# Two-layer hybrid decoder trunk on one core: attention's transposes moved into the projection, fewer modulation tiles ahead of the norm, decay rows split in two, and the second layer's w2 products as three single passes

## The reference

```python
for l in range(DEPTH):                                        # DEPTH = 2
    mod = (silu(c) @ w_ada[l] + b_ada[l])[:, None, :]         # w_ada: 1024 x 6144
    sh1, sc1, g1, sh2, sc2, g2 = jnp.split(mod, 6, axis=-1)
    u = layer_norm(x) * (1.0 + sc1) + sh1
    z = u @ w_in[l]                                           # 2920 columns, four head groups
    y_a = mla_mixer(...)          # 4 heads, latent attention, width 96
    y_b = mlstm_mixer(...)        # 4 heads, q k^T times exp(decay), causal
    y_c = short_conv_mixer(...)   # b * conv3(c * h), 256 channels
    y_d = diff_attn_mixer(...)    # 4 heads, two softmax maps each, width 32
    mix = jnp.concatenate([y_a, y_b, y_c, y_d], axis=-1) @ w_out[l]
    x = layer_norm(DN_ALPHA * x + g1 * mix) * ln1_g[l] + ln1_b[l]
    u2 = layer_norm(x) * (1.0 + sc2) + sh2
    ffn = grouped_moe(u2, w_router, b_router, w1[l], w3[l], w2[l])
    #     16 experts of hidden width 256: w2[e] @ (silu(w1[e] u) * w3[e] u), top 2 of one group of 4
    x = layer_norm(DN_ALPHA * x + g2 * ffn) * ln2_g[l] + ln2_b[l]
```

## Time and profile before

| what | value |
|---|---|
| median of 3 runs | 805.85 us (802.21 to 807.32) |
| the profiled execution: its own time | 810.88 us |
| its span, first to last instruction | 809.0 us |
| TensorE busy | 682.6 us (84%) |
| VectorE busy | 570.6 us (71%) |
| ScalarE busy | 331.4 us (41%) |
| GpSimd busy | 71.9 us (9%) |
| mean granted TensorE clock | 0.916 |
| DMA over the span | 192.39 MB, 238 GB/s |

### The profile page before, as it was taken

One profiled execution on the slowest core, in us unless ns is written; L12 is line 12 of the kernel. 1 busy time (PEld: TensorE's weight loads), 2 busy tenths in 40 slices (PEclk: granted clock), 3 DMA queues, 4 the chain that ended last, 5 costly groups with the idle time before them and its releaser, 6 DMA issues.

```text
span 809.0 us, 9622 instructions
## 1 busy us (share of the span) xinstructions
PE 682.6 (84%) x3630; PEld 543.7 (67%) x3630; DVE 570.6 (71%) x808; ACT 331.4 (41%) x511; POOL 71.9 (9%) x40
## 2 busy tenths in 40 slices
PE   1379898989549899999964999899866899999991
PEld 1379886769448566676644998776866666666650
DVE  6796986565878676766559998656577767665527
ACT  0154445630244544545223455374045444544510
POOL 3001000530100000000112000044010000000001
PEclk9998999889759999999975999989976999999996
DMA  9979977005614899999690993530152789998811
GB/s 347 380 230 318 315 259 285 2 1 183 255 58 153 293 396 368 396 376 380 227 366 19 311 375 151 183 130 1 53 201 112 257 293 410 359 383 307 276 53 54
DMA packets 81701, 192.39 MB, mean 238 GB/s; under 512 B 10984, under 2 KB 42984, under 8 KB 81644
## 3 DMA queue, kind: packets, MB, share of 16 engines
q1 hardware_dynamic: 75240, 184.73, 62.4%
q10 hardware_dynamic: 6408, 6.96, 2.9%
HBM read 190.60 MB, written 1.05 MB: 237 GB/s over the span
## 4 chain that ended last, share of the span: by engine, by line
PE 72%; DVE 15%; issue 4%; DMA 3%; ACT 3%; POOL 2%; POOLq 0%; ACTq 0%; SPq 0%; DVEq 0%
PE bank L1823 21%; PE bank L1876 13%; PE bank L1543 11%; PE bank L1541 7%; PE bank L1697 2%; PE bank L1910 2%; DVE mod_acc L945 2%; DMA ada_ring<-in_w_ada 1%; DVE st L956 1%; POOL rstd L585 1%; DMA ada_open<-in_w_ada 1%; DVE e_lo L1046 1%; PE bank L1807 1%; DVE us_rest L1420 1%; PE bank L1507 1%
## 5 line engine op out<-in xcount | busy, mean ns | idle before, releaser
L1046 DVE TENSOR_TENSOR e_lo<-e_ring,e_hi 128x2048 fp32r<-128x2048 f32 x64 | 146.6, 2291 | 76.4 <-ACT e_hi L657 76.4
L657 ACT ACTIVATE e_hi<-e_ring 128x2048 fp32r<-128x2048 f32 x64 | 122.1, 1908 | 2.3 <-DMA e_ring<-in_w 2.3
L1876 PE MATMUL bank<-e_ring,hT 128*128 128x512 f32 x256 | 115.3, 593 | 2.3 <-ACT hT L875 2.3
L1823 PE MATMUL bank<-e_hi,us_hi 128*128 128x512 f32 x256 | 102.0, 406 | 0.0
L1823 PE MATMUL bank<-e_hi,us_lo 128*128 128x512 f32 x256 | 98.9, 395 | 0.0
L945 DVE SCALAR_TENSOR_TENSOR mod_acc<-ada_ring,c_col,mod_acc 128x1024 f32<-128x1024 f32 x59 | 74.2, 1281 | 21.2 <-DMA ada_ring<-in_w_ada 21.2
L1876 PEld LDWEIGHTS bank<-e_ring,hT 128*128 128x128 f32 x256 | 48.1, 189 | 51.1 <-issue 49.1
L1543 PE MATMUL bank<-w_hi,u_hi 128*128 128x256 f32 (+2 forms) x224 | 66.6, 297 | 8.3 <-DVE u_lo L1065 7.2
L1823 PE MATMUL bank<-e_lo,us_hi 128*128 128x512 f32 x256 | 69.8, 395 | 0.0
L1543 PE MATMUL bank<-w_lo,u_hi 128*128 128x256 f32 (+2 forms) x224 | 66.0, 295 | 0.0
L1543 PE MATMUL bank<-w_hi,u_lo 128*128 128x256 f32 (+2 forms) x224 | 65.8, 294 | 0.0
(11 more groups left out here) (267 smaller groups left out, 1392.4 us busy)
## 6 DMA issues: line engine op xcount, KB each, us to landing
e_ring<-in_w SPq DMA_DIRECT2D x128, 512.0 KB, 5.9
e_ring<-in_w SPq DMA_DIRECT2D x32, 1024.0 KB, 8.1
ada_ring<-in_w_ada SPq DMA_DIRECT2D x59, 512.0 KB, 8.1
w_ring<-in_w_in SPq DMA_DIRECT2D x20, 1024.0 KB, 8.0
ada_open<-in_w_ada SPq DMA_DIRECT2D x37, 512.0 KB, 8.8
w_ring<-in_w_out SPq DMA_DIRECT2D x8, 1024.0 KB, 5.0
w_ring<-in_w_in SPq DMA_DIRECT2D x2, 1056.0 KB, 5.8
ln_gb<-in_ln_g ACTq DMA_DIRECT2D x4, 512.0 KB, 4.1
```

The source lines that it names most:

```text
L657: nc.scalar.activation(e_hi[slot][:], e_ring[E_RAW[c % len(E_RAW)]][:], ACT.Copy).then_inc(e_hi_ready, 1)
L1046: V.tensor_tensor(e_lo[slot][:], e_ring[slot][:], e_hi[E_HIGH[c % len(E_HIGH)]][:].bitcast(F32), ALU.subtract).then_inc(e_lo_ready, 1)
L1823: return pe.matmul(dst, u[:, k, cols], w[:, :, k % (KC // 2), :], start=start, stop=stop)
L1876: mm = pe.matmul(bank[banks[half]][:, :], hT[:, c * P:(c + 1) * P], w[:, c, half * 512:(half + 1) * 512], start=(start and c == 0), stop=( ...
```

## The change

1. `turn_rows` moves behind tile 10, and `turn_diff` and `turn_qk` between the two halves of tile 11; `turn_qk` writes other banks. `gate_rows` goes behind `scores(1)`. ScalarE's and VectorE's parts move along. The convolution is cut into five steps, one behind each of the pairs 0 to 4.
2. `ADA_EARLY` is 5. Three of the tiles go where the eight stood, two between the first and second half of `post_norm` for t = 0. Layer 1 takes 5 of its 8 `gate2` tiles there as well and the other three with experts 0 to 2. In layer 0 eleven go with experts 8 to 15, two each with 13 to 15.
3. The decay rows are split into `rows_hi` and `rows_lo`, and the float32 product with `head_sel` becomes two fp32r products with a broadcast column of the identity. The banks of the score pairs swap, so that map 12 waits for ten exponentials and map 13 for twelve.
4. W_out's fourth low part moves from GpSimd to VectorE, behind pair 5; its four high pieces (12 to 15) follow piece 11 directly on ScalarE.
5. In layer 1 w2 and hT are split: `down_high` on ScalarE, `down_low` and `hidden_low` on VectorE, and `expert_down` runs 12 single-pass matmuls in place of 4 float32 ones. `down_hi` lies over `mod_acc`, `down_lo` in the slot of w2 itself.

The core of the diff; banks, buffer addresses and semaphore counts are left out.

```diff
-ADA_EARLY = 8
+ADA_EARLY = 5
...
+def ada_beside(l, e):
+    late = ADA_FIRST - ADA_EARLY if l < DEPTH - 1 else 0
+    done = 0 if l < DEPTH - 1 else ADA_EARLY
+    double = max(0, late - (N_EXP - KC))
+    lo = done + e + max(0, e - (N_EXP - double))
+    hi = lo + (2 if e >= N_EXP - double else 1)
+    return range(ADA_AT["last", l] + lo, ADA_AT["last", l] + min(hi, KC + late))
...
         def score_bank(at):
-            return (0 if at // 2 % 2 else 2) + at % 2
+            return (2 if at // 2 % 2 else 0) + at % 2
...
                 root(2, slice(0, 8))
-                out_low(W_OUT_TILES - 1)
...
+            def down_high(l, e):
+                act.wait_ge(*arrivals["down", l, e])
+                if e >= 2:
+                    act.wait_ge(*layer_view(l)(down_done, e - 1))
+                nc.scalar.activation(down_hi[e % 2][:], e_ring[E_DOWN[e % 2]][:, 0:2 * D].rearrange("p (c n) -> p c n", c=2),
+                                     ACT.Copy).then_inc(down_hi_ready, 1)
...
+                        if step == 2 * NW_IN - 1:
+                            d_out_all()
+                            turned_queries_out()
                         act.wait_ge(*Y(z_done, step + 1))
...
-                    if n == 11:
-                        d_out_all()
+                    if n == 10:
+                        rows_and_lambda()
...
-                    out_high(at)
+                    for piece in range(at, at + 1 if at < 11 else 16 if at == 11 else at):
+                        out_high(piece)
...
+                split_down = l == DEPTH - 1
+                if split_down:
+                    act.wait_ge(*Y(row2_done, 4))
+                    act.wait_ge(*Y(rows_g, 2))
+                    down_high(l, 0)
...
                         turned_out(e)
                         if 2 * e + 4 < N_CHUNKS:
                             up_high(l, 2 * e + 4)
+                        if split_down and e + 1 < N_EXP:
+                            down_high(l, e + 1)
...
                 for half in range(2):
+                    if t == 0 and half == 1 and gate == 0:
+                        for i in ada_early(l)[ADA_SLOTS:]:
+                            ada_step(i)
                     half_done(t, half)
...
+                decays = rows[:, :, :].rearrange("p a b -> p (a b)")[:, P:4 * P]
+                link(V.tensor_copy(rows_hi[:], decays))
+                V.tensor_tensor(rows_lo[:], decays, rows_hi[:].bitcast(F32), ALU.subtract)
...
+                    if p <= 4:
+                        conv_step(p)
...
                     if p == 5:
                         diff_out(1)
+                        dve.wait_ge(*Y(out_hi_ready, W_OUT_TILES * W_OUT_PIECES))
+                        V.tensor_tensor(w_lo[3][:, :, 0:256], w_ring[3][:, :, 0:256],
+                                        w_hi[W_OUT_HIGH[3]][:].bitcast(F32)[:, :, 0:256], ALU.subtract).then_inc(out_lo_last, 1)
...
-                    for i in range(ADA_EARLY):
-                        ada_step(ADA_AT["next"] + i)
+                for i in ada_early(l)[:ADA_SLOTS]:
+                    ada_step(i)
...
+                split_down = l == DEPTH - 1
+                if split_down:
+                    down_low(0)
...
                             up_low(l, 2 * e + 3)
                         if e % 4 == 0 and e > 0:
                             group_out(e // 4 - 1)
+                        hidden_low(e)
                         if 2 * e + 4 < N_CHUNKS:
                             up_low(l, 2 * e + 4)
-                        ada_beside(e)
+                        if split_down and e + 1 < N_EXP:
+                            down_low(e + 1)
+                        ada_steps(e)
...
-                    for i in range(2):
-                        causal(bank[2 * i])
                     for i, h in enumerate(heads):
-                        pe.matmul(bank[2 * i][:, 0:384], head_sel[:, h * P:(h + 1) * P], decays, start=False, stop=True)
+                        pe.wait_ge(*(Y(p_act, 10 + 2 * i) if p == 6 else Y(decay_ready, i + 1)))
+                        causal(bank[2 * i])
+                        for q, part in enumerate((rows_hi, rows_lo)):
+                            pe.matmul(bank[2 * i][:, 0:384], head_r[:, h:h + 1].to_broadcast([NH, P]), part[:, :], start=False, stop=(q == 1))
...
+                if split_down:
+                    pe.wait_ge(down_hi_ready, e + 1)
+                    passes = ((hT_hi, down_hi[e % 2]), (hT_lo, down_hi[e % 2]), (hT_hi, down_lo[E_DOWN[e % 2]]))
...
+                        if n == NW_IN - 1 and half == 1:
+                            turn_diff()
+                            turn_qk()
                         w_step(l, n, half)
...
-                    if n == 11:
-                        turn_diff()
+                    if n == 10:
                         turn_rows()
-                pe.wait_ge(*Y(z_out, 21))
-                turn_qk()
-                gate_rows()
                 for p in range(NPAIR + 2):
                     if p < NPAIR:
                         scores(p)
+                    if p == 1:
+                        gate_rows()
```

218 lines of the change are left out of this document (126 added, 92 removed).

## The result

After the change the kernel takes 819.71 us (median of 4 runs, 812.62 to 824.98); the kernel before, on the same chip, 804.17 (802.21 to 807.32). The ratio is 1.017, with an interval of 1.012 to 1.022; it leaves out the longest of the four, which fell in a slower state of the chip (817.88 is the median of the other three). The prediction was 782.2.

A forecast was written before the change was run, and what follows sets the result against it. TensorE, busy 84% of the span and 72% of the chain, was taken to bound the kernel where it arrives last. 810.9 - 16.4 - 8.3 + 1.1 = 787.3; from the median, 805.85 - 23.6 = 782.2 us; range 768 to 797.

The forecast's parts named there:

- Part 5: Layer 1's experts: single-pass w2 products, TensorE's saving mostly taken by a new two-expert load loop; +1.1 us net.
- load 4.9: Layer 1's w2 loop: each w2 load lands in 4.9 us, within 18.2 us for two experts.
- rivals D: Layer 1's w2 loop: landings of 6 to 7 us add some 10 us, with rival C besides; 799 us, chance 0.08.
- rival E: Layer 1's w2 loop: landings stay 8.4 us and the clock falls; +29 against -24.7, 810 us, chance 0.04.
- the start costs: Layer 1's first experts: early low parts delay 3.4 us, expert 3's queued load 2.7 us.
- -5: Layer 1's experts: TensorE's work beside the loop, scatter and second gate's rows, gains 7.2 us, of which 5 counted.
- Parts 2 and 3: Attention, both layers: low part off GpSimd gives 2.5 us a layer; split decays 1.4, less 0.2 for splitting rows.
- The convolution's steps fit VectorE's gaps: Opening of attention: the convolution steps fit because VectorE is busy only 4.04 of 9.60 us.
- rival C: Attention: GpSimd holds the moved low part and the clock stays low; gain 5 us a layer, 788.6 us, chance 0.16.
- The decays and the clock: Attention, per layer: split decay product brings the last pair's products 1.4 us earlier; fewer TensorE waits raise the clock, 1.5.
- Parts 1 and 4: Opening of attention: first scores 3.7 us earlier, 3.0 net a layer; layer 0's norm: last half 8.3 us earlier.
- The sum: Whole kernel: attention 16.4 us over both layers and norm 8.3 gained, layer 1's experts +1.1; 23.6 us off the median.

The follow-up runs named there:

- both passes moved: Changed kernel with part 5 undone, convolution's five steps behind pairs 0 and 1, fourth low part behind the last y_lo: 793.4 us, ratio 0.986.
- the runs that had each alone: Kernel before with only the fourth low part moved to VectorE behind the last y_lo: 803.2 us, 0.998; with only part 4's modulation tiles: 796.53 us, 0.993.

## Why the prediction was wrong, step by step

**Part 5 failed, in two terms.** The loop of two experts was drawn rightly, "followed from the end of one expert's down products", and the trace after shows it link by link; "load 4.9" was mis-sized. It came from a load at 754.42 us, late in the layer, and stood for all. The landings on the chain are 9.1, 7.2, 6.8 and 6.7 us up to 727 us, so that two experts take 20.2 us and not 18.2. The text had a longer landing in its rivals D ("landings of 6 to 7 us") and E ("it decides from landings of about 8 us on"), and argued against E that landings fall to 4.9 once the modulation tiles end. The trace of the kernel before already shows otherwise. Its last modulation tile was issued at 703.05; this is the w2 load issued at 714.76, behind it (DMA issues of before, 714.5 to 715.5 us):

```profile
e_ring<-in_w SPq DMA_DIRECT2D x1, 1024.0 KB, 7.0
```

The next, at 723.89, took 7.0 as well, and only those from 735.30 on took 4.9 to 5.2. Nor does a long landing need the uneven traffic of the loop: in the fastest version on SyncE's queue, where the experts follow evenly, w2 landed after 5.5 to 8.5 us from 640 to 732 us, and no wait for it is on the chain.

The second term is "the start costs", 3.4 + 2.7 = 6.1 us. By the start of expert 4's up products the changed kernel has lost 11.8 us (16.5 + 25.9 against 12.4 + 18.3, in the chains). The clock falls are in it, which the forecast left to rival E: the up products of experts 1, 2 and 4 take 7.20, 7.46 and 6.47 us for 5.47, together 4.7. From there to the start of expert 15's the change loses 2.5 us against the version with w2 unsplit, where the forecast, with its "-5", had a gain; and from there to the end another 2.0, for which the forecast had no term (expert 15 too waits there for its w2: 4.88 us to land, then the high pass). Together part 5 costs 15 to 16 us and not 1.1.

**Parts 2 and 3 failed in attention.** "The convolution's steps fit VectorE's gaps" counted VectorE's busy time (4.04 of 9.60) and not GpSimd's in the same row, 4.52 us: a step in a gap is no use where GpSimd's pass fills that gap. The text held this very thing against the low part (rival C), and did not ask it of the convolution, whose operations are of the same kind. By the Trainium skill ("GPSIMD Engine Reference", 1. Specifications) an instruction with two SBUF inputs on VectorE contends with GpSimd for shared interfaces; L1254 and L1360 are both of that kind, so the trace agrees, with 3.71 us for 0.87 and 4.65 for 2.29. For the low part the forecast had 0.4 us if it is held and 2.9 if not, and took 1.4 a layer; the held case came. Moving both gives 10 us, and by the profiles that is the low part's gain; the convolution met the pass again.

**The decays and the clock** were 1.4 and 1.5 us a layer. No gain of the split shows in the times. The low stretches stayed as long as TensorE idled there: granted clock 0.83 and 0.73 from 148 to 170 us after, 0.64 and 0.70 in the earlier trace rows. From 158 us on it came to 1.00 with the low part moved (0.83 from 138 to 158 us even there).

**Parts 1 and 4 were right**: the first scores 3.9 us a layer nearer in the traces for 3.7, and the norm's last half at TensorE's end. Part 4 measured 6.0 us for 8.3, within its interval.

**The sum.** The parts without w2 were to give 24.7 us. They give 1.4 as written, and 11.1 with both passes moved. Of the 13.6 that are missing even then, part 2 is some 3 and part 4 some 2, by the runs that had each alone. The sum had no term for the convolution held 4.2 us a layer. The decays (2.8) and the clock (3.0) no run isolates well enough to say. So the rest stays open.

The fastest version is the one with w2 split late, its third pass last and the low part clear of GpSimd: 0.982 of before, or 0.979 with the w2 loads on ScalarE's queue. The split of w2 is not where its gain is shown to come from; the version without it is at 0.986.

## What to carry to other kernels

When a buffer's reader is moved ahead, draw the loop that starts at the release of the buffer and give the load its longest landing, not its shortest: here the landing went from 4.9 to 9.1 us with what else was in flight, and it can be read off the kernel before at the same place in its stream. When work is moved to an idle engine, look at what its neighbours do in those same microseconds; here two operations of 0.9 us cost 3.7 if GpSimd has a pass under way, and moving them earlier only made another one meet it. Look at the trace after such a move before crediting it. Cost the beginning of a pipeline on its own: most of the loss here fell in the first four of sixteen experts.

## What the runs showed of the hardware

**VectorE beside GpSimd looks stopped, not slowed.** The 4.65 us of the low part are 2.5 up to the end of GpSimd's pass and 2.1 behind it, with 2.29 of work. The operation of 0.69 us that took 4.91 ended 0.55 behind the pass (143.92 against 143.37), and line 1243 of before 0.55 behind its own. So each did some 0.14 us of its work at the start and all the rest when the pass was over, however long the pass still had. The first of the two convolution operations (L1254) took 3.31 us for 0.48 and ended 0.3 behind. VectorE's other operations in the same stretch, which read a bank of PSUM, were of their usual length (L1343, 0.55 us). The chain of waits calls the stop "issue".

**A long landing is not cured by another queue.** Up to some 760 us, with at least two other loads in flight at its issue, 1 MB landed after 5.5 to 10.0 us on ScalarE's queue (issued at once) and after 5.3 to 9.1 us on SyncE's (the changed kernel); with at most one in flight it was 4.9 to 5.0 us on either.

**The clock decides 4 us of a projection by chance.** The first 288 matmuls of layer 0's projection took 35.4 to 35.9 us in nine of the sixteen profiles and 39.1 to 39.9 in seven, and layer 1's first 336 took 41.0 to 41.5 in nine and 45.5 to 45.7 in seven, with the same code. Busy time by stretch at the start of layer 0's projection, of the kernel before and of the one with the fourth low part moved:

```profile
40.00:45.00 5.00, 0.32 (x3) 0.22 (x2) 4.25 (x12) 4.30 (x13) 0.00 (x0) 1.00 1.07 385
...
60.00:65.00 5.00, 5.00 (x26) 5.00 (x26) 4.93 (x15) 1.86 (x3) 2.80 (x2) 0.53 0.90 306
```
```profile
40.00:45.00 5.00, 0.32 (x2) 0.21 (x2) 4.33 (x12) 4.39 (x13) 0.00 (x0) 0.50 1.06 381
...
60.00:65.00 5.00, 5.00 (x45) 5.00 (x44) 4.93 (x15) 1.98 (x3) 2.82 (x2) 1.00 1.05 387
```

TensorE was all but idle ahead of both. In the first the clock fell in the middle of the projection, to 0.79 and 0.53 from 55 to 65 us, though TensorE was busy without a gap there (0.50 is 1.2 GHz, 1.00 is 2.4). All seven long profiles show such a fall, and none of the nine short ones. The clock ahead of the projection doesn't decide it: of the seven profiles in which it was at 1.00 from 40 to 45 us three are short, and of the nine in which it was at 0.50 three are long. Why it falls the profiles don't show. Two such places make 8 us between executions of one kernel, which is why stages, and not whole spans, were compared, and why the differences below 1% above carry wide intervals.
